# State-space mixer in sub-chunks of four tokens: recurrence over 64 steps, lag matrices, rotations on VectorE

## What is computed

```python
bu_re = jnp.einsum('bsgc,gpc->bsgp', ug, bb_re)      # bu_im likewise
_, _, xs_re, xs_im = lax.associative_scan(combine, (a_re, a_im, bu_re, bu_im), axis=1)
y = (jnp.einsum('bsgp,gcp->bsgc', xs_re, c_re) - jnp.einsum('bsgp,gcp->bsgc', xs_im, c_im))
y = jax.nn.gelu(y.reshape(bsz, seq, S5_WIDTH) + d_skip * uf)
y = y * jax.nn.sigmoid(y @ w_glu)
```

## Time and profile before

| | us |
|---|---|
| median of 3 runs | 1339.41 (1338.76 to 1341.43) |
| profiled execution, its own time | 1337.92 |
| its span, first to last instruction | 1336.4 |
| mixers up to the chunk recurrence | 0 to 269.7 |
| chunk recurrence, output projection, router | 269.7 to 363.7 |
| expert loop | 363.7 to 1293.5 |
| tail | 1293.5 to 1336.4 |

### The profile page before, as it was taken

One profiled execution on the slowest core, in us unless ns is written; L12 is line 12 of the kernel. 1 busy time (PEld: TensorE's weight loads), 2 busy tenths in 40 slices (PEclk: granted clock), 3 DMA queues, 4 the chain that ended last, 5 costly groups with the idle time before them and its releaser, 6 DMA issues. The chain is left out here.

```text
span 1336.4 us, 18328 instructions
## 1 busy us (share of the span) xinstructions
PE 1175.0 (88%) x7685; PEld 507.5 (38%) x7686; DVE 476.5 (36%) x749; ACT 209.5 (16%) x324; POOL 145.2 (11%) x60
## 2 busy tenths in 40 slices
PE   5794751599499999999999999999999999999997
PEld 4473541574233333333333333333333333333333
DVE  6699979925712121211211211121121212112122
ACT  3341210122601010001110001011000100100023
POOL 3087528400200000000000000000000000000000
PEclk9796965799799999999999999999999999999998
DMA  9200210232489999999999999999999999999970
GB/s 332 86 1 0 95 37 0 112 119 95 154 355 430 427 430 429 428 431 426 430 429 427 431 428 428 430 426 430 428 428 431 426 430 429 428 431 426 430 306 31
DMA packets 44361, 429.84 MB, mean 322 GB/s; under 512 B 4816, under 2 KB 15440, under 8 KB 19760
## 3 DMA queue, kind: packets, MB, share of 16 engines
q1 hardware_dynamic: 44016, 428.43, 76.6%
q0 software_dynamic: 320, 1.05, 0.2%
HBM read 428.42 MB, written 1.05 MB: 321 GB/s over the span
## 5 line engine op out<-in xcount | busy, mean ns | idle before, releaser
L1070 PE MATMUL bank<-arena 128*64 128x512 f32 (+5 forms) x5387 | 920.0, 478 | 24.7 <-DMA arena<-in_exp_w_up 19.1
L1070 PEld LDWEIGHTS bank<-arena 128*64 128x64 f32 (+4 forms) x5388 | 316.2, 128 | 604.9 <-issue 541.8
L207 PE MATMUL bank<-arena 64*64 64x64 f32 (+4 forms) x1552 | 159.9, 301 | 54.2 <-DVE arena L707 45.2
L207 PEld LDWEIGHTS bank<-arena 64*64 64x64 f32 (+2 forms) x1552 | 123.0, 175 | 90.7 <-DVE arena L707 46.5
L1320 DVE COPY arena<-bank 128x512 f32<-128x512 f32 x32 | 22.1, 692 | 234.9 <-PE bank L1070 234.9
L1261 ACT ACTIVATE arena<-arena 128x512 f32<-128x512 f32 x32 | 20.2, 631 | 515.3 <-DVE arena L1305 515.3
L1310 DVE TENSOR_SCALAR arena<-bank 128x512 f32<-128x512 f32 x32 | 22.1, 692 | 211.5 <-PE bank L1070 211.5
L1305 DVE TENSOR_SCALAR arena<-bank 128x512 f32<-128x512 f32 x32 | 22.1, 692 | 188.8 <-PE bank L1070 188.8
L1264 ACT ACTIVATE arena<-bank 128x256 f32<-128x256 f32 x32 | 12.3, 384 | 309.7 <-PE bank L1360 309.7
L1281 DVE TENSOR_TENSOR arena<-bank,par 128x512 f32<-128x512 f32 x33 | 22.8, 692 | 76.4 <-PE bank L1070 76.4
L207 PE MATMUL bank<-arena,con 128*128 128x256 f32 (+1 forms) x32 | 15.9, 641 | 31.6 <-ACT arena L418 18.8
(11 more groups left out here) (250 smaller groups left out, 654.3 us busy)
## 6 DMA issues: line engine op xcount, KB each, us to landing
arena<-in_exp_w_gate SPq DMA_DIRECT2D x64, 2048.0 KB, 23.4
arena<-in_exp_w_down SPq DMA_DIRECT2D x64, 2048.0 KB, 21.8
arena<-in_exp_w_up SPq DMA_DIRECT2D x64, 2048.0 KB, 25.3
arena<-in_w_in SPq DMA_DIRECT2D x8, 1024.0 KB, 12.2
arena<-in_w_out SPq DMA_DIRECT2D x4, 1024.0 KB, 7.4
arena<-in_ple_w_gate SPq DMA_DIRECT2D x2, 2048.0 KB, 21.7
arena<-in_xT SPq DMA_DIRECT2D x1, 1024.0 KB, 5.8
arena<-in_lora SPq DMA_DIRECT2D x1, 1024.0 KB, 13.0
```

The source lines that it names most:

```text
L207: return nc.tensor.matmul(out, lhsT, rhs, start=start, stop=stop, skip_group_check=True)
L1070: return nc.tensor.matmul(out, lhsT, rhs, start=start, stop=stop, skip_group_check=True)
```

## The change

The state-space recurrence runs over sub-chunks of `SUB` = 4 tokens: 64 steps instead of 256. The state is carried from sub-chunk to sub-chunk only, and the four tokens inside are handled by matrices.

- DVE computes powers of a up to the fourth, G = a^n B for n = 0 to 3 and O = C a^n for n = 1 to 4 (`products`, twice six operations of 128x1024), and one table angle over 64 steps for all 16 tiles. ACT spreads G and O into zeroed block-diagonal tiles (`gpad`, `opad`), which POOL cleared with memsets.
- PE forms the lag matrices C a^n B (`kernel_taps`, 64 matmuls 32 or 96 wide), transposes G (`turn_g`, 32 transposes), stacks the four tokens of u on the partitions (`stack_u`, 64 matmuls 32x64) and multiplies (`into`, 2 x 16 matmuls 128x64). ACT copies the results out of PSUM (L412, L417, L420).
- The rotations `phase_off` and `phase_on` run on DVE, in two halves H of 128x512 operands; POOL's 48 operations of 128x1024 are gone. Two scans of 128x512 for each half take the place of 32 scans of 128x256.
- `s5_out(g)` has 4 wide matmuls with the lag matrices and 32 matmuls of 32x63; it runs in levels 0 to 3, and `s5_y(g)` one level later.
- `project(2)` is followed by the new PE work, and ACT takes the copy of `project(3)` behind it. `params` is now SP's first DMA. Two parts of `w_out` are fetched after the last `s5_out` and no longer after the last projection.

```diff
@@ gpsimd
+                nc.gpsimd.memset(un(45), 0.0).then_inc(s["pads_clear"], 1)
+                nc.gpsimd.memset(un(16, 4), 0.0).then_inc(s["pads_clear"], 1)
+                nc.gpsimd.memset(un(20, 4), 0.0).then_inc(s["pads_clear"], 1)
                 pool.wait_ge(s["dh_ready"], 1)
...
-                for g in (0, 2):
-                    phase_off(g)
-                    phase_off(g + 1)
-                    phase_on(g)
-                    phase_on(g + 1)
+                pool.wait_ge(s["proj_done"], 2)
+                nc.gpsimd.memset(un(2, 2), 0.0).then_inc(s["pads_clear"], 1)
@@ scalar, behind lora1
+                lora_out(0)
+                for m in range(2):
+                    act.wait_ge(s["g_built"], m + 1)
+                    for g in range(2):
+                        A(gpad[m][a, :, :, o].rearrange("p j n c -> p n j c"), gprod[m][a], ACT.Copy).then_inc(s["g_padded"], 1)
+                lora_out(1)
+                for m in range(2):
+                    act.wait_ge(s["o_built"], m + 1)
+                    for g in range(2):
+                        A(opad[m][a, :, :, o], oprod[m][a], ACT.Copy, scale=(1.0, -1.0)[m]).then_inc(s["o_padded"], 1)
+                lora_out(2)
+                act.wait_ge(s["table_arg"], 1)
+                A(tcos[:, :, :], tsin[:, :, :], ACT.Sin, scale=0.5)
+                A(tsin[:, :, :], tsin[:, :, :], ACT.Sin).then_inc(s["table_ready"], 1)
...
                 copy_proj(2)
+                act.wait_ge(s["taps_done"], 1)
+                for j in range(4):
+                    last = A(taps[a, :, :, a], banks[7][a, :]..., ACT.Copy)
+                for m in range(2):
+                    for q in range(4):
+                        act.wait_ge(s["g_turned"], 4 * m + q + 1)
+                        A(gturn[m][:, 4 * q:4 * q + 4, :], banks[2 + q % 2]..., ACT.Copy).then_inc(s["g_copied"], 1)
+                for b in range(2):
+                    act.wait_ge(s["stacked"], b + 1)
+                    A(ustack[:, 8 * b:8 * b + 8, :], banks[2 + b]..., ACT.Copy).then_inc(s["ustack_ready"], 1)
                 act.wait_ge(s["decay_ready"], 1)
@@ vector
+                def phase_off(H):
+                    dve.wait_ge(s["into_done"], H + 1)
+                    dve.wait_ge(s["table_ready"], 2)
+                    dve.wait_ge(s["proj_done"], (4, 7)[H])
+                    tt(zs[0], zr, c, ALU.mult)
+                    tt(hs[H][0], zi, sn, ALU.mult)
+                    tt(zs[1], zi, c, ALU.mult)
+                    link(tt(hs[H][1], zr, sn, ALU.mult))
+                    tt(zs[0], zs[0], hs[H][0], ALU.add).then_inc(s["phase_off"], 1)
+                    tt(zs[1], zs[1], hs[H][1], ALU.subtract).then_inc(s["phase_off"], 1)
+                def phase_on(H):
+                    for m in range(2):
+                        z = V.tensor_tensor_scan(un((10, 12)[H])[:, m * 512:m * 512 + 512], mag, un(11)[:, m * 512:m * 512 + 512], 0.0, ALU.mult, ALU.add)
+                    link(z)
+                    tt(zs[0], hs[H][0], c, ALU.mult)
+                    link(tt(zs[1], hs[H][1], sn, ALU.mult))
...
@@ vector, main list
-                scan(0)
                 dve.wait_ge(s["proj_copied"], 4)
                 link(token_shift("k", kx))
...
-                scan(1)
+                phase_off(0)
                 dve.wait_ge(s["kk_root"], 1)
...
-                table_arg(2)
+                phase_on(0)
                 dve.wait_ge(s["proj_copied"], 6)
                 link(token_shift("r", rr))
...
-                table_cos(2)
+                phase_off(1)
...
-                scan(2)
+                phase_on(1)
                 for lev in range(LEVELS):
...
-                    if lev == 0:
-                        scan(3)
-                    if lev in (2, 3):
-                        s5_y(lev)
+                    if lev:
+                        s5_y(lev - 1)
@@ tensor
-                project(2, 1)
+                project(2)
+                kernel_taps()
+                turn_g()
+                stack_u()
                 project(3)
+                into(0)
+                into(1)
                 project(4)
...
+                        if m == 1:
+                            pe.wait_ge(s["phase_off"], 4)
...
-                    if lev in (2, 3):
+                    if lev < FT:
                         s5_out(lev)
+                def s5_out(g):
+                    for n in range(SUB):
+                        mm(bank[:, n * NK:T], taps[:, g, n, :], uP[:, g, 0:SUB - n, :], n == 0, False)
+                    for r in range(SUB):
+                        for m in range(2):
+                            for i in range(4):
+                                last = mm(bank[32 * i:32 * i + 32, r * NK + 1:(r + 1) * NK], opad[m][:, r, j, :],
+                                          hs[g // 2][m][:, j % 8, 0:NK - 1], False, r == SUB - 1 and m == 1)
```

More of the change, by code:

```diff
@@ L263, in _ @@
                 sp.dma_start(wout[0][:, :, :], wo[0]).then_inc(wout_in, 16)
-                sp.wait_ge(s["phase_on"], 4)
                 sp.wait_ge(s["s5_out_done"], 4)
+                for c in (1, 2):
+                    sp.dma_start(wout[c][:, :, :], wo[c]).then_inc(wout_in, 16)
+                sp.wait_ge(s["scaled"], 3)
                 for c in (0, 4, 5):
@@ L372, in bu_copy @@
-                def bu_copy(g):
-                    for j in range(4):
-                        act.wait_ge(s["bu_done"], 4 * g + j + 1)
-                        if g >= 2 and j == 0:
-                            act.wait_ge(s["phase_on"], g - 1)
-                        A(sA[g % 2][:, j, :], banks[2 + j % 2][:, 0:T], ACT.Copy)
-                        A(sB[g % 2][:, j, :], banks[2 + j % 2][:, T:2 * T], ACT.Copy).then_inc(s["bu_copied"], 1)
-                table_angle(0)
-                table_angle(1)
@@ L391, in _, with lora_out @@
[L391 removed]
+                    A(dst, src, ACT.Copy).then_inc(s["proj_copied"], 1)
+                def lora_out(m):
+                    dst, bias = ((lw, "w0"), (la, "a0"), (lg, None))[m]
                     if m == 0:
@@ L406, in _ @@
                             last.then_inc(s["lora2_copied"], 1)
-                table_sin(1)
-                bu_copy(1)
-                act.wait_ge(s["lora1_done"], 3)
-                copy_proj(2)
+                for n in range(2):
+                    copy_proj(n)
+                act.wait_ge(s["lora1_done"], 2)
+                A(lora_hidden[0:CH, 0:T], banks[4][0:CH, 0:T], ACT.Tanh)
+                A(lora_hidden[CH:P, 0:T], banks[4][CH:P, 0:T], ACT.Copy).then_inc(s["lora_hidden_ready"], 1)
@@ L768, in _, with project @@
                 last.then_inc(s["rms_summed"], 1)
-                def bu_tile(g, j):
-                    if g == 0 and j == 0:
-                        pe.wait_ge(s["bb_copied"], 2)
-                        pe.wait_ge(s["proj_copied"], 2)
-                    if g >= 2 and j == 0:
-                        pe.wait_ge(s["s5_y"], g - 1)
-                    if 4 * g + j >= 2:
-                        pe.wait_ge(s["bu_copied"], 4 * g + j - 1)
-                    a = slice(32 * j, 32 * j + 32)
-                    for m in range(2):
-                        last = mm(banks[2 + j % 2][:, m * T:(m + 1) * T], bb[a, m, g * P:(g + 1) * P], uT[a, g, :], True, True)
-                    last.then_inc(s["bu_done"], 1)
-                def project(n, group=None):
+                def project(n):
                     q = order[n]
@@ L793, in project, with kernel_taps @@
                             last = mm(banks[n % 2][:, f * T:(f + 1) * T], win[q][:, k, f * P:(f + 1) * P], hT[:, k, :], k == 0, k == KD - 1)
-                            if group is not None and k % 4 == 1:
-                                bu_tile(group, 2 * f + k // 4)
                     last.then_inc(s["proj_done"], 1)
-                def s5_out(g):
-                    pe.wait_ge(s["phase_on"], g + 1)
-                    pe.wait_ge(s["bu_copied"], min(4 * g + 8, 16))
-                    for j in range(4):
-                        a = slice(32 * j, 32 * j + 32)
-                        for m, src in enumerate((sT1[g % 2], sT2[g % 2])):
-                            last = mm(banks[2 + g % 2][a, 0:T], cc[:, m, (4 * g + j) * 32:(4 * g + j + 1) * 32], src[:, j, :], m == 0, m == 1)
+                def kernel_taps():
+                    pe.wait_ge(s["cpad_ready"], 4)
+                    pe.wait_ge(s["g_padded"], 4)
+                    pe.wait_ge(s["o_padded"], 4)
+                    pe.wait_ge(s["lora_hidden_ready"], 2)
+                    for j in range(NJ):
+                        a, o = slice(32 * (j % 4), 32 * (j % 4) + 32), P * (j // 4)
+                        for m in range(2):
+                            mm(banks[7][a, o:o + 32], gpad[m][:, j, 0, :], cpad[:, m, j, :], j < 4 and m == 0, m == 1)
+                            last = mm(banks[7][a, o + 32:o + P].rearrange("p (n c) -> p n c", c=32), gpad[m][:, j, 0, :],
```

(15 more changed lines are left out.)

347 lines of the change are left out of this document (179 added, 168 removed).

## The result

| | before | after |
|---|---|---|
| median, us | 1339.3 (1338.76 to 1341.43, 4 runs) | 1266.85 (1265.17 to 1267.35, 4 runs) |
| span of the profiled execution | 1336.4 | 1265.3 |

The ratio is 0.9454, with a 95% interval of 0.9438 to 0.9470: 72.5 us less, against a forecast of 1276 in a range of 1260 to 1296. The direction, the range and the place of the gain were right. The number was 9 us too high and lay nearly at that of rival C (1266).

What follows compares the result with a forecast made beforehand. DVE, slowed by turns with POOL, was taken to bound the mixers, with the expert loop only shifting. 1336.4 + 2 - 1.6 - 64.2 + 2 = 1274.6 us span, + 1.5 outside it = 1276; range 1260 to 1296.

Steps and rivals of the forecast that it cites:

- rival C: Relay ahead of the shift of k is shorter because the clock stays full and handovers overlap: -10 us, 1266; chance 0.12.
- What bounds: DVE bounds the mixers from 94.0 to 269.7 us, much of it turns with POOL; the expert loop only shifts.
- Part 1: Start, up to 38.7 us: POOL's memsets hold DVE's tensor_scalar instructions until 12 us; cost +2 us (0 to +15).
- Rival B: Start: memsets at POOL's reading rate hold DVE's chain to 24.6 us; +13 us, 1289; chance 0.08.
- Part 2: From 38.7 us to the token shift of k: new PE and ACT relay eats most of what is freed; -1.6 us.
- Rival A: Relay and levels PE-bound: narrow matmuls into one 32-column group cannot overlap, clock halves in gaps; +19 us, 1295; chance 0.17.
- rule against the change: Some 62 us [sic, ns] per matmul without hardware decoding: 512 narrow instructions would cost 10 us more; not added.
- Part 3: Shift of k to the chunk recurrence: DVE's list at undisturbed durations takes 111.5 us in place of 175.7; -64.2 us.
- Part 4: Behind the recurrence's start: same instructions, late `w_out` parts have time enough; 0 us, perhaps -1.5 from the first chunk.
- Handovers: Handing over between engines, which the sum rounds away; +2 us.
- D: Slower than before: every narrow instruction waits for its own weights; at 0.2 us each 1356 us; chance 0.02.
- E: Turns with POOL are not lost time, only scans and tables go; about -25 us, 1313; chance 0.01.

Runs made afterwards that it cites:

- e7_groups: Changed kernel with matmul order altered: `stack_u` stays in one group of 32 output partitions for eight matmuls, `kernel_taps` goes round the four groups; 1270.99 us.
- e9_pe_busy: Changed kernel plus matmuls with unused results on PE, 11 behind level 4 and 3 ahead of the second variance matmul; 1262.94 us.
- e10_order2: Changed kernel reordered: `project(3)` and `project(4)` directly behind `project(2)`, with ScalarE copies, shift of v, `s5_y(3)` and large memsets moved; 1249.79 us.
- e4_load_write: Changed kernel plus 72 POOL memsets of 128x1024, which write SBUF and read nothing; 1269.47 us.

## Why the prediction was right, and where it was off

**What bounds.** Right: DVE's lengthened instructions were the lost time. The long rows of before come to some 62 us over the plain ones; narrowing POOL's operations gave 59.8 (DVE busy 61.0 us less), adding 28 to the changed kernel cost 44.

**Part 1**, +2: measured +1.6, of which 1.1 by the mechanism given. Rival B's slow memsets fall (3.53 us for 4096 columns).

**Part 2**, -1.6: measured -6.1. The path was right (the shift of k waits for the copy of `project(3)`, L358; DVE idle 22.8 us, 27 forecast). The failed terms are the narrow matmuls: `kernel_taps` 4.4 us where I had 7, `stack_u` 2.0 where I had 5.5. I had priced them per instruction from the 64x64 row. Rival A's text had the right variable, whether neighbours share a 32-column group, but the sum did not use it: in `e7_groups`, where they share it, `stack_u` takes 6.0 us, near my 5.5. These two terms make 6.1 us; the part came out only 4.5 us shorter than forecast, since `project(3)` took 8.2 us for 7.0 (a gap of 0.9 in it), and some 0.4 us are in the rest of the relay. None of this ran near the price per instruction of the rule against the change: `stack_u` took 0.016 us each.

**Part 3**, -64.2: measured -69.3. The wait for the norm was 5.15 us for 5.4. `phase_off(1)` ended 45.5 us behind the shift's start (46.7 forecast), the scores to the end of `phase_on(1)` took 22.0 (24.0). From the end of `phase_on(1)` to the recurrence it took 38.9 us, forecast 41. Together that makes the 5.1. Inside the last term two errors partly cancel. The levels were 10.1 apart (10.5), and of the 5 us for handing over in level 1 only 1.4 existed: I had let PE and DVE take turns where PE had 2 us of slack, so levels 1 to 3 took 31.7 us for 36.5. But three times 10.5 and 5 are already 36.5 of the 37 us in the sum, which leaves 0.5 for level 4 and the gelu; they took 3.3.

**Part 4**, 0: measured +2.7. This step failed in sign. I took the stage as unchanged because its instructions are, and even allowed for a gain; but its clock depends on how PE spends the time ahead. `e9_pe_busy` gives it back and 0.9 us more. The late parts of `w_out` were not tried apart; no wait for them shows.

**Handovers**, +2: not there; the measured parts leave no rest. Together 1276 - 0.4 - 4.5 - 5.1 + 2.7 - 2 = 1266.7.

**Rivals.** C came nearest in its number and partly in its reason (handovers overlap), but the clock did not stay full (0.93 in the relay, 0.89 to the recurrence, 0.86 behind it), and its 10 us were all put on the relay, which gave 4.5; that it hit 1266 is mostly luck. A's price was wrong: the narrow matmuls cost less than assumed, and doubling them in the levels costs nothing. D and E never came near.

## What to carry to other kernels

Where POOL and DVE both read two SBUF operands, compare the same DVE shape with POOL idle and busy: the difference times the count is what moving or shrinking POOL's work can give, and moving it at full length may give little. Narrow matmuls that go round the 32-partition output groups run beside each other; write the loops that way, though here it moved the whole kernel's time by nothing that could be told. A gap on PE can be paid twice, as the gap and as half clock behind it (5.3 us was, in the changed kernel; 1.4 us in `e10_order2` was not), so when an order changes, look at the granted clock of the stage behind as well, even where no instruction of it was touched.

## What the hardware showed that I had not expected

- More work made the kernel faster: 14 unused matmuls gave 3.9 us. Doubled narrow matmuls cost nothing; of the 3.4 us that the kernel came out faster some 1.0 was there ahead of the edit.
- Three POOL memsets in a row let a waiting DVE instruction of 16 columns wait for all of them (8.70 us), while POOL's multiplications let one DVE instruction in after each. So did the memsets of `e4_load_write` (four DVE instructions in 4.04 us). These and the multiplications have a semaphore step between one and the next (`link`), the three in a row have none; whether that is the reason was not tested.
- Beside POOL's reads a DVE operation with one SBUF and one PSUM input keeps its 0.68 us, one with two SBUF inputs of the same size takes 2.54 to 2.83.
